# Two heads on halves of TensorE's array, one item for the compressed branch, and GpSimd on part of the probabilities

## The chip, the cores and the metric

The kernel runs on one core of one Trainium2 chip. Its time is the device time of one execution in microseconds. TensorE is called PE below, its weight loads PEld, VectorE DVE, ScalarE ACT, GpSimd POOL, and the queue that issues most DMAs SP. The profile is one execution recorded by the hardware profiler.

## The reference

The function is two blocks, one after the other, on x of 256 tokens by 1024. The first block has two layers of feed-forward networks and a mixer each (a gated recurrence in one, latent attention in the other); the change leaves it alone. The second block has two layers, each a modulated norm, a projection of 1024 to 3864 columns, the hybrid attention below, an output projection and a gated residual. With 256 tokens, 8 "moba" heads of width 64 see their own keys under a causal mask, and 8 "NSA" heads in two groups of four share keys and values per group, in three branches that are weighted by sigmoid gates and added:

```python
s_own = jnp.einsum('hqd,hkd->hqk', q, k_own).astype(jnp.float32)           # moba: causal, minus slope * distance
s_c = jnp.einsum('gjqd,gtd->gjqt', qg, kcb).astype(jnp.float32)            # compressed: T = 15 keys for each group
p_c = jax.nn.softmax(s_c, axis=-1) * ok_c
o_c = jnp.einsum('gjqt,gtd->gjqd', p_c.astype(vcb.dtype), vcb)
o_n = g[..., 0:1] * o_c + g[..., 1:2] * o_s + g[..., 2:3] * o_w            # o_s selected, o_w window
y = jnp.concatenate([o_m * jax.nn.silu(zm), o_n * jax.nn.silu(zn)], axis=-1)
return y @ w_out
```

At this length all 4 blocks of the selected branch are chosen and the window covers all keys, so both are plain causal attention with their own keys and values.

## The kernel before

Activations lie as features on 128 partitions by 256 tokens. Weights stream from memory in chunks of 128 x 2048; ACT rounds each half of a chunk (128 x 1024) to fp32r (`hi`, L688) and DVE forms the rest (`lo`, L1717), and a product of the large projections is three fp32r matmuls (L1049 to L1051). The order on each engine is written out by hand, and engines wait on counted steps of one another; nothing reorders it.

The change is in the second block, whose two layers run one after the other. After the projection each layer has an attention stage over a list `ITEMS`: 4 moba items, then for each of 4 pairs of NSA heads a window, a selected and a compressed item, 16 in all. An item is a pair of heads of width 64 that lie on partitions 0 to 63 and 64 to 127. Since the array is used whole, the keys of each head stand in a buffer that is zero in the other head's rows (`kmz`, `ksz`, `kwz`), and the values in one that is zero in the other head's columns (`vmz`, `vsz`, `vwz`). POOL writes these zeros at the layer's start (L643).

An item passes through these steps:

- PE, `scores_c`: for each of the two row tiles of 128 tokens, one fp32 matmul against both heads' keys (L1617: 256 columns for tile 0, 512 for tile 1) and one bf16 matmul that adds the bias (L1619). An fp32 matmul shows as two records, each with its own weight load.
- DVE, `maxima_c`: the negated row maxima, a reduction for each row tile (L2102).
- ACT, `exps`: four exponentials from PSUM, with sums (L928).
- DVE, `weigh_c`: reciprocal of the sums (L2111), for NSA times the gate (L2117), then four products in place (L2122).
- PE, `transposes_c`: six transposes (L1456). ACT copies the result to `ptC` (L935).
- PE, `values_c`: for each head 256 columns (L1650) and 128 columns (L1651), all fp32.
- After a pair's last item: DVE multiplies with z (L2293), ACT and DVE split the product (L1006, L2300).

A compressed item has 15 keys for each head: scores of 30 columns (L1607, L1609), four exponentials of 15 columns, four 16-row transposes (L1630) and products with 15 rows (L1645).

The loop on PE is, for item i: scores of i+2, values of i-1, transposes of i. On ACT: exps of i, in items 4 to 11 one half of the output weights, the two copies of i-1, the split of i-3. On DVE: weigh of i, the product of i-2, maxima of i+2, the split of i-3, in items 4 to 11 one half of the weights. In the last turns PE also takes the first parts of the output projection (`wout`), and the rest follows.

## Time and profile before

| what | value |
|---|---|
| median of 3 runs | 1602.69 us (1594.97 to 1605.1) |
| the profiled execution's own time | 1599.1 us |
| its span, first to last instruction | 1597.3 us |
| granted TensorE clock, mean | 0.983 |
| PE busy | 1519.2 us (95%), 12299 matmul records |
| DVE / ACT / POOL busy | 1105.5 / 779.5 / 202.8 us |
| attention stage, layer 0 | scores from 1301.90, last but one transposes end at 1360.32 us |
| attention stage, layer 1 | the same from 1499.07 to 1556.05 us |

The two stages make 115.4 us of the span. PE's busy time is not a measure of its work, since records overlap: the work of a group of matmuls is read from the start of one to the start of the next. A granted clock of 1.00 is the level of 2.4 GHz and 0.50 that of 1.2 GHz.

### The profile page before, as it was taken

The page shows a single profiled execution, that of the slowest core. Times are in us where ns is not written, and L with a number is a line of the kernel's source. Part 1 is how long each engine was busy: PE and PEld are TensorE (multiplying, and loading weights), DVE is VectorE, ACT ScalarE, POOL GpSimd, SP SyncE. Part 2 cuts the span into 40 slices and gives each one's busy share as a digit, 9 for nine tenths or more (in the row PEclk, how much of TensorE's full clock was granted, in tenths as well). Part 3 has the DMA queues.
Part 4 walks back from the last instruction along what each step waited for, and adds up shares of the span by engine and source line. Part 5 has one row for each costly group of instructions (what it writes and reads, how often), then busy time and mean ns, then how long its engine had stood idle before and what let it go on. Part 6 is the DMA issues. An engine that isn't in the chain of part 4 may idle for free.

```text
span 1597.3 us, 31108 instructions
## 1 busy us (share of the span) xinstructions
PE 1519.2 (95%) x12299; PEld 1460.1 (91%) x12299; DVE 1105.5 (69%) x1648; ACT 779.5 (49%) x1259; POOL 202.8 (13%) x239
## 2 busy tenths in 40 slices
PE   6999998989999989999999999999987998989998
PEld 6999998989999989999989799999977976889767
DVE  5886559966886586876677745976578448394583
ACT  5554375355544356544352634544364338254481
POOL 1111015601421010111010001101023000120000
PEclk9999999999999999999999999999998999999999
DMA  7787744325776645766645254876555503085010
GB/s 225 223 273 244 232 133 133 111 75 169 248 245 215 226 124 177 256 222 200 223 116 149 80 159 152 276 233 212 180 158 159 162 27 106 1 239 174 14 54 27
DMA packets 219309, 264.86 MB, mean 166 GB/s; under 512 B 22253, under 2 KB 197325, under 8 KB 219213
## 3 DMA queue, kind: packets, MB, share of 16 engines
q1 hardware_dynamic: 209136, 234.58, 47.0%
q0 software_dynamic: 8960, 27.37, 5.2%
q10 hardware_dynamic: 1117, 1.57, 0.3%
q8 instruction: 67, 1.10, 0.3%
q14 instruction: 29, 0.24, 0.0%
HBM read 262.44 MB, written 1.05 MB: 165 GB/s over the span
## 4 chain that ended last, share of the span: by engine, by line
PE 79%; DVE 11%; ACT 5%; DMA 2%; issue 1%; POOL 0%; SPq 0%; DVEq 0%; ACTq 0%
PE bank L1049 23%; PE bank L1051 23%; PE bank L1050 23%; DVE w_lo L1717 4%; PE bank L1617 2%; PE bank L1456 1%; PE bank L1650 1%; DVE rs L1729 1%; ACT w_hi L688 1%; DVE hg_s L1917 1%; PE bank L1470 1%; PE bank L1468 1%; PE bank L1063 1%; ACT sC L928 1%; DMA w_raw<-in_ffn_w_in 1%
## 5 line engine op out<-in xcount | busy, mean ns | idle before, releaser
L688 ACT ACTIVATE w_hi<-w_raw 128x1024 fp32r<-128x1024 f32 x452 | 454.3, 1039 | 466.0 <-PE bank L1051 312.4
L1049 PE MATMUL bank<-xh,w_lo 128*128 128x256 f32 x2312 | 652.5, 282 | 24.5 <-DVE xl L2176 14.2
L1717 DVE TENSOR_TENSOR w_lo<-w_raw,w_hi 128x1024 fp32r<-128x1024 f32 x452 | 549.4, 1251 | 148.5 <-ACT w_hi L688 147.4
L1050 PE MATMUL bank<-xl,w_hi 128*128 128x256 f32 x2312 | 647.8, 280 | 0.0
L1051 PE MATMUL bank<-xh,w_hi 128*128 128x256 f32 x2312 | 647.7, 280 | 0.0
L1049 PEld LDWEIGHTS bank<-xh,w_lo 128*128 128x128 f32 x2312 | 438.1, 189 | 28.9 <-DVE xl L2176 14.9
L1050 PEld LDWEIGHTS bank<-xl,w_hi 128*128 128x128 f32 x2312 | 437.4, 189 | 1.1 <-issue 0.7
L1051 PEld LDWEIGHTS bank<-xh,w_hi 128*128 128x128 f32 x2312 | 436.9, 189 | 0.3
L1049 PE MATMUL bank<-hh,w_lo 128*128 (+1 forms) x704 | 194.7, 277 | 0.0
L1050 PE MATMUL bank<-hl,w_hi 128*128 (+1 forms) x704 | 194.3, 276 | 0.0
L1051 PE MATMUL bank<-hh,w_hi 128*128 (+1 forms) x704 | 194.3, 276 | 0.0
L531 POOL DMA_DIRECT2D mod_raw<-in_w_ada x128 | 69.0, 543 | 529.6 <-DVE mod_acc L1749 401.8
L1050 PEld LDWEIGHTS bank<-hl,w_hi 128*128 128x128 f32 x704 | 132.1, 188 | 0.0
L1049 PEld LDWEIGHTS bank<-hh,w_lo 128*128 128x128 f32 x704 | 132.1, 188 | 0.0
L1051 PEld LDWEIGHTS bank<-hh,w_hi 128*128 128x128 f32 x704 | 132.1, 188 | 0.0
L1749 DVE SCALAR_TENSOR_TENSOR mod_acc<-mod_raw,csf,mod_acc 128x384 f32<-128x384 f32 x112 | 65.3, 619 | 38.0 <-DMA mod_raw<-in_w_ada 37.5
L610 POOL TENSOR_TENSOR sq<-sq 128x1024 f32<-128x1024 f32 x7 | 16.9, 2407 | 404.3 <-ACT sq L706 404.3
L699 ACT ACTIVATE xh<-X,col 128x256 fp32r<-128x256 f32 x72 | 30.4, 496 | 52.4 <-PE bank L1051 36.0
L928 ACT ACTIVATE sC<-bank,nmC 128x256 f32<-128x256 f32 (+2 forms) x128 | 48.0, 411 | 9.0 <-DVE nmC L2102 8.9
L653 POOL TENSOR_TENSOR y<-y,rs 128x512 f32<-128x512 f32 x4 | 6.9, 1738 | 355.6 <-DVE rs L1729 355.6
L1773 DVE TENSOR_TENSOR gate_t<-bank,rs 128x512 f32<-128x512 f32 x44 | 30.3, 689 | 27.7 <-PE bank L1051 27.6
L1781 DVE TENSOR_TENSOR up_t<-bank,rs 128x512 f32<-128x512 f32 x44 | 30.3, 688 | 24.7 <-PE bank L1051 24.7
(367 smaller groups left out, 2213.4 us busy)
## 6 DMA issues: line engine op xcount, KB each, us to landing
w_raw<-in_ffn_w_in SPq DMA_DIRECT2D x176, 512.0 KB, 4.7
w_raw<-in_ffn_w_out SPq DMA_DIRECT2D x88, 512.0 KB, 4.4
w_raw<-in_w_in SPq DMA_DIRECT2D x52, 512.0 KB, 4.5
mod_raw<-in_w_ada POOLq DMA_DIRECT2D x128, 192.0 KB, 4.4
w_raw<-in_a_w_in SPq DMA_DIRECT2D x32, 512.0 KB, 4.5
w_raw<-in_ple_w_gate SPq DMA_DIRECT2D x16, 512.0 KB, 4.5
w_raw<-in_b_w_out SPq DMA_DIRECT2D x16, 512.0 KB, 3.6
w_raw<-in_w_out SPq DMA_DIRECT2D x16, 512.0 KB, 3.5
```

The costliest lines, as they stand in the source:

```text
L531: pool.dma_start(mod_raw[:, n % 2, :], io["w_ada_2"][l][P * k:P * (k + 1), col:col + MOD_COLS]).then_inc(sem[f"mod_landed{n % 2}"], 16)
L688: A(w_hi[:, c % NSLOT, cols], w_raw[:, c % NRAW, cols], ACT.Copy).then_inc(*did(hi_ready))
L699: A(xh[:, k, :], X[:, k, :], ACT.Copy, scale=gain(k)).then_inc(*did(act_steps, ("xh", nu, k)))
L928: A(s[:, h, cols], src, ACT.Exp, bias=nm[:, 2 * t + h:2 * t + h + 1], accum_out=den[:, 2 * t + h:2 * t + h + 1]).then_inc(*did(act_steps, ...
L1049: mm(out, lhs[1], rhs[0], start=start, stop=False, skip_group_check=skip)
L1050: mm(out, lhs[0], rhs[1], start=False, stop=False, skip_group_check=skip)
L1051: return mm(out, lhs[0], rhs[0], start=False, stop=stop, skip_group_check=skip)
L1617: mm(bank[b][:, 0:2 * n], q[:, m, t * P:(t + 1) * P], kz[:, :, 0:n], start=True, stop=False)
L1717: V.tensor_tensor(w_lo[:, c % NSLOT, cols], w_raw[:, c % NRAW, cols], f32(w_hi[:, c % NSLOT, cols]), ALU.subtract).then_inc(*did(lo_ready))
L1749: V.scalar_tensor_tensor(acc, raw, cs, acc, ALU.mult, ALU.add).then_inc(sem["mod_steps"], 1)
L1773: V.tensor_tensor(gate_t[:, p % 2, :, :], two(bank[b][:, :]), rep(rs[:, :], 2), ALU.mult).then_inc(*did(gate_scaled))
L1781: V.tensor_tensor(up_t[:, p % 2, :, :], two(bank[b + 1][:, :]), rep(rs[:, :], 2), ALU.mult).then_inc(*did(up_scaled))
```

## The change

The keys and values no longer stand between zeros (`km`, `ksd`, `kwd`, `vmt`, `vst`, `vwt`). A score matmul has one head's 64 rows of queries and keys, and writes a PSUM bank of its own; a value matmul has one head's 64 output columns and writes 64 partitions. The shapes place them on row halves (64 x 128 at rows 0 or 64) and on column halves (128 x 64 at columns 0 or 64) of the array. The biases stay on the whole array, as four matmuls in place of two.

The compressed branch of all 8 heads and both row tiles is one item, the fifth of 13: one bias matmul, 8 score matmuls of 30 columns, one maximum, one subtraction, one exponential, one set of weights, two transposes, one copy. Its value product is a matmul with 32 rows inside each selected item (`vcz`, `ptK`); to this end the compressed values are computed for 4 copies of the 15 keys (`ghr`).

POOL multiplies the probabilities of row tile 1 of both heads (2 x 256 columns) by their weights, and DVE those of row tile 0 (2 x 128). The zeroing of the padded buffers is gone, and each of the copies into them is one instead of several.

```diff
 
-    ITEMS = [("moba", m, True, True) for m in range(4)]
+    ITEMS = [("moba", m, True, True) for m in range(4)] + [("cmp", 0, False, False)]
     for m in range(4):
-        ITEMS += [("win", m, True, False), ("slc", m, False, False), ("cmp", m, False, True)]
...
             pool.wait_ge(*when(("x", 9 + l, 3)))
-            for z in (kmz, vmz, ksz, kwz, vsz, vwz, kcz, vcz):
...
+
+            for i, (kind, _, _, _) in enumerate(ITEMS):
+                if kind != "cmp":
+                    item = ("c", l, i)
+                    pool.wait_ge(*when(("weight", item)))
+                    t1 = sC[:, i % 3, :, P:3 * P]
+                    G.tensor_tensor(t1, t1, rdC[:, i % 3, 2:4].unsqueeze(2).to_broadcast([P, 2, T]), ALU.mult).then_inc(*did(pool_steps, ("probs1", item)))
...
-                probs_t(("c", l, i), ptC[:, i % 2], 2 * P if kind == "cmp" else 3 * P)
+                item = ("c", l, i)
+                if ITEMS[i][0] != "cmp":
+                    return probs_t(item, ptC[:, i % 2], 3 * P)
+                act.wait_ge(*when(("pt", item)))
+                A(ptK[:, :], bank[4][:, 0:T], ACT.Copy).then_inc(*did(act_steps, ("ptcopy", item)))
...
-                exps(("c", l, i), 2 * (i % 2), sC[:, i % 3], nmC[:, i % 3], denC[:, i % 3], CMP_T if kind == "cmp" else None)
+                if kind == "cmp":
+                    act.wait_ge(*when(("max", ("c", l, i))))
+                    A(sC[:, i % 3, 0, 0:T], sC[:, i % 3, 0, 0:T], ACT.Exp).then_inc(*did(act_steps, ("exps", ("c", l, i))))
+                else:
+                    exps(("c", l, i), 2 * (i % 2), sC[:, i % 3], nmC[:, i % 3], denC[:, i % 3])
...
-            last.then_inc(*did(pe_groups, ("vcmp", l)))
+            pe.wait_ge(*when(("ghr", l)))
+            mm(bank[2][:, 0:DH], ghr[:, :], wc2[:, 2, :], start=True, stop=True).then_inc(*did(pe_groups, ("vcmp", l)))
...
                 if kind == "cmp":
                     take(b0)
+                    mm(bank[b0][:, 0:T], ident_bf[:, :], cbias[:, :, :, :].rearrange("p t h n -> p (t h n)"), start=True, stop=False, skip_group_check=True)
                     for t in range(TB):
-                        last = mm(bank[b0][:, t * 2 * CMP_T:(t + 1) * 2 * CMP_T], q[:, m, t * P:(t + 1) * P], kcz[:, g, :, 0:CMP_T], start=True, stop=False)
-
-                        last = mm(bank[b0][:, t * 2 * CMP_T:(t + 1) * 2 * CMP_T], ident_bf[:, :], cbias[:, 2 * m:2 * m + 2, t, :], start=False, stop=True)
+                        for mk in range(4):
+                            col = t * P + 32 * mk
+                            last = mm(bank[b0][:, col:col + 32].rearrange("p (h n) -> p h n", h=2)[:, :, 0:CMP_T], qs[:, mk, t * P:(t + 1) * P],
+                                      kcz[:, mk // 2, :, 0:CMP_T], start=False, stop=(t == 1 and mk == 3), skip_group_check=True)
                     last.then_inc(*did(pe_groups, ("s", ("c", l, i), 1)))
-                    release[b0] = ("exps", ("c", l, i))
+                    release[b0] = ("max", ("c", l, i))
...
-                kz = {"moba": kmz[:, m], "slc": ksz[:, g], "win": kwz[:, g]}[kind]
+                keys = {"moba": km[:, m], "slc": ksd[:, g], "win": kwd[:, g]}[kind]
+                for h in range(2):
+                    take(b0 + h)
+
                 for t in range(TB):
-                    b, n = b0 + t, (t + 1) * P
-                    take(b)
-                    mm(bank[b][:, 0:2 * n], q[:, m, t * P:(t + 1) * P], kz[:, :, 0:n], start=True, stop=False)
-
-                    mm(bank[b][:, 0:2 * n], ident_bf[:, :], bias[:, 2 * m:2 * m + 2, T - n:T], start=False, stop=True).then_inc(*did(pe_groups, ("s", ("c", l, i), t)))
-                    release[b] = ("exps", ("c", l, i))
+                    for h in range(2):
+                        rows_ = slice(h * DH, (h + 1) * DH)
+                        mm(bank[b0 + h][:, t * P:t * P + (t + 1) * P], q[rows_, m, t * P:(t + 1) * P], keys[rows_, 0:(t + 1) * P],
+                           start=(t == 0), stop=False, skip_group_check=True)
+                for t in range(TB):
+                    for h in range(2):
+                        last = mm(bank[b0 + h][:, t * P:t * P + (t + 1) * P], ident_bf[:, :], bias[:, 2 * m + h, T - (t + 1) * P:T],
+                                  start=False, stop=True, skip_group_check=True)
+                last.then_inc(*did(pe_groups, ("s", ("c", l, i), 1)))
+                for h in range(2):
+                    release[b0 + h] = ("exps", ("c", l, i))
...
             def transposes_c(i):
+                item = ("c", l, i)
                 if ITEMS[i][0] != "cmp":
-                    return transposes(("c", l, i), sC[:, i % 3])
...
+                    return transposes(item, sC[:, i % 3])
+                take(4)
+                pe.wait_ge(*when(("probs", item)))
+                for t in range(TB):
+                    last = nc.tensor.transpose(bank[4][:, t * P:(t + 1) * P], sC[:, i % 3, 0, t * P:(t + 1) * P], ident)
+                release[4] = ("ptcopy", item)
+                last.then_inc(*did(pe_groups, ("pt", item)))
...
                 kind, m, start, stop = ITEMS[i]
+                if kind == "cmp":
+                    return
...
-                o = bank[b][:, 0:T]
-                for h in range(2):
-                    if kind == "cmp":
-                        last = mm(o, vcz[0:CMP_T, g, h, :], ptC[0:CMP_T, i % 2, h, 0:T], start=False, stop=(h == 1), skip_group_check=True)
-                        continue
-                    v = {"moba": [vmz[:, t, 2 * m + h, :] for t in range(TB)],
-                         "slc": [vsz[:, t, g, h, :] for t in range(TB)], "win": [vwz[:, t, g, h, :] for t in range(TB)]}[kind]
-
-                    block0 = lambda: mm(o, v[0], ptC[:, i % 2, h, 0:T], start=(start and h == 0), stop=(stop and h == 1), skip_group_check=True)
-                    block1 = lambda: mm(o[:, P:T], v[1], ptC[:, i % 2, h, T:T + P], start=False, stop=False, skip_group_check=True)
-                    for product in ((block0, block1) if h == 0 else (block1, block0)):
-                        last = product()
+                for t in range(TB):
+                    for h in range(2):
+                        v = {"moba": vmt[:, t, 2 * m + h, :], "slc": vst[:, t, g, :], "win": vwt[:, t, g, :]}[kind]
+                        rows_, cols = slice(h * DH, (h + 1) * DH), slice(t * P, T)
+                        last = mm(bank[b][rows_, cols], v, ptC[:, i % 2, h, t * T:T + t * P], start=(start and t == 0), stop=(kind == "moba" and t == 1), skip_group_check=True)
+                if kind == "slc":
+                    rows_ = slice(32 * m, 32 * m + 32)
+                    last = mm(bank[b][:, 0:T], vcz[rows_, :, :].rearrange("p h d -> p (h d)"), ptK[rows_, :], start=False, stop=True, skip_group_check=True)
...
-            for which, kz in ((0, ksz), (1, kwz)):
+            for which, kd in ((0, ksd), (1, kwd)):
                 here, there = kA[:, 2 + which, :], bank[1][:, which * T:(which + 1) * T]
                 for g in range(GROUPS):
                     for h in range(2):
                         rows_ = slice(h * DH, (h + 1) * DH)
-                        V.tensor_copy(kz[rows_, g, h, :], (here if g == h else there)[rows_, :]).then_inc(*did(dve_steps, ("kB_used", l, 1)))
+                        V.tensor_copy(kd[rows_, g, :], (here if g == h else there)[rows_, :]).then_inc(*did(dve_steps, ("kB_used", l, 1)))
+            dve.wait_ge(*when(("gelu", l)))
+            for g in range(GROUPS):
+                V.tensor_copy(ghr[:, 64 * g:64 * g + 64].rearrange("p (a n) -> p a n", n=16)[:, :, 0:CMP_T],
+                              rep(gh[:, 30 + 15 * g:45 + 15 * g], 4)).then_inc(*did(dve_steps, ("ghr", l)))
             dve.wait_ge(*when(("kcmp", l)))
...
             for h in range(2):
-                V.tensor_copy(vcz[0:CMP_T, :, h, h * DH:(h + 1) * DH], bank[2][0:CMP_T, 0:P].rearrange("p (g d) -> p g d", g=GROUPS)).then_inc(*did(dve_steps, ("vcz", l)))
+                V.tensor_scalar(vcz[:, h, :], bank[2][:, 0:DH], const[:, C_HALF + h:C_HALF + h + 1], None, ALU.mult).then_inc(*did(dve_steps, ("vcz", l)))
...
                 dve.wait_ge(*when(("s", item, 1)))
-                for t in range(TB):
-                    V.tensor_reduce(nm[:, 2 * t:2 * t + 2], two(bank[b0][:, 30 * t:30 * t + 30]), AX.X, ALU.max, negate=True).then_inc(*did(dve_steps, ("max", item)))
+                if ITEMS[i][0] != "cmp":
+                    for t in range(TB):
+                        V.tensor_reduce(nm[:, 2 * t:2 * t + 2], twin[i % 2][:, :, t * P:t * P + (t + 1) * P], AX.X, ALU.max, negate=True).then_inc(*did(dve_steps, ("max", item)))
+                    return
+
+                rows16 = bank[2 * (i % 2)][:, 0:T].rearrange("p (a n) -> p a n", n=16)
+                nm16 = nmK[:, :, :].rearrange("p t h -> p (t h)")
+                V.tensor_reduce(nm16, rows16, AX.X, ALU.max, negate=True).then_inc(*did(dve_steps))
+                dve.wait_ge(*did.last)
+                dve.wait_ge(*when(("pt", ("c", l, i - 3))))
+                V.tensor_tensor(s_[:, 0, 0:T].rearrange("p (a n) -> p a n", n=16), rows16, nm16.unsqueeze(2).to_broadcast([P, 16, 16]), ALU.add).then_inc(*did(dve_steps, ("max", item)))
...
+                dve.wait_ge(*when(("exps", item)))
+                if kind == "cmp":
+                    s16 = s_[:, 0, 0:T].rearrange("p (a n) -> p a n", n=16)
+                    V.tensor_reduce(nmK[:, :, :].rearrange("p t h -> p (t h)"), s16, AX.X, ALU.add).then_inc(*did(dve_steps))
...
+                    dve.wait_ge(*did.last)
+                    V.tensor_tensor(s16, s16, rdK[:, :, :].rearrange("p t h -> p (t h)").unsqueeze(2).to_broadcast([P, 16, 16]), ALU.mult).then_inc(*did(dve_steps, ("probs", item)))
+                    return
+
+                V.reciprocal(rd[:, :], den[:, :]).then_inc(*did(dve_steps, ("weight", item)))
                 if kind != "moba":
-                    branch = {"cmp": 0, "slc": 1, "win": 2}[kind]
-                    gate = gates[:, :, :].rearrange("p t (h b) -> p t h b", b=3)[:, :, 2 * m:2 * m + 2, branch]
-                weigh(("c", l, i), sC[:, i % 3], denC[:, i % 3], rdC[:, i % 3], gate, kind == "cmp", CMP_T if kind == "cmp" else None)
+                    dve.wait_ge(*did.last)
+                    branch = {"slc": 1, "win": 2}[kind]
+                    V.tensor_tensor(two(rd[:, :]), two(rd[:, :]), gates4[:, :, 2 * m:2 * m + 2, branch], ALU.mult).then_inc(*did(dve_steps, ("weight", item)))
+                dve.wait_ge(*did.last)
+                for h in range(2):
+                    V.tensor_scalar(s_[:, h, 0:P], s_[:, h, 0:P], rd[:, h:h + 1], None, ALU.mult).then_inc(*did(dve_steps, ("probs", item)))
```

The order on PE before, one turn of the attention loop: scores of a selected item (`ksz`: its keys), value products of the selected item before (`ptC`, `vsz`: transposed probabilities and values), transposes of a compressed one.

```order
L1617 MATMUL bank<-ksz,qs 128x256
L1619 MATMUL bank<-bias,ident_bf 128x256
L1617 MATMUL bank<-ksz,qs 128x512
L1619 MATMUL bank<-bias,ident_bf 128x512
L1650 MATMUL bank<-ptC,vsz 128x256
L1651 MATMUL bank<-ptC,vsz 128x128 x2
L1650 MATMUL bank<-ptC,vsz 128x256
L1630 MATMUL bank<-const,sC 16x128 x4
```

The order on PE now, one turn in which the value products of a selected item come with the 32-row product of the compressed branch (L1682; `kwd`: keys of a window item, `vst`: values of the selected one):

```order
L1643 MATMUL twin<-kwd,qs 128x128 x2
L1643 MATMUL twin<-kwd,qs 128x256 x2
L1647 MATMUL twin<-bias,ident_bf 128x128 x2
L1647 MATMUL twin<-bias,ident_bf 128x256 x2
L1679 MATMUL twin<-ptC,vst 64x256 x2
L1679 MATMUL twin<-ptC,vst 64x128 x2
L1682 MATMUL twin<-ptK,vcz 128x256
L1478 MATMUL twin<-const,sC 128x128 x6
```

The order of the stages in a turn is the same; inside it the matmuls of the two heads alternate, and both row tiles' scores stand ahead of the biases.

The order on DVE before, the turn of the first selected item of a layer:

```order
L2111 RECIPROCAL rdC<-denC 128x4 [waits lo_ready,act_steps]
L2117 TENSOR_TENSOR rdC<-rdC,gates 128x4 [waits dve_steps]
L2122 TENSOR_SCALAR sC<-sC,rdC 128x128 [waits dve_steps]
L2122 TENSOR_SCALAR sC<-sC,rdC 128x256
L2122 TENSOR_SCALAR sC<-sC,rdC 128x128
L2122 TENSOR_SCALAR sC<-sC,rdC 128x256
L2293 TENSOR_TENSOR yC<-bank,zm 128x256 [waits dve_steps,pe_groups]
L2102 TENSOR_REDUCE nmC<-bank 128x2 [waits pe_groups] x2
L2300 TENSOR_TENSOR xl<-yC,xh 128x256 [waits act_steps]
L1717 TENSOR_TENSOR w_lo<-w_raw,w_hi 128x1024 [waits hi_ready]
```

And now, the turn of the first window item:

```order
L2315 RECIPROCAL rdC<-denC 128x4 [waits act_steps]
L2319 TENSOR_TENSOR rdC<-rdC,gates 128x4 [waits dve_steps]
L2322 TENSOR_SCALAR sC<-sC,rdC 128x128 [waits dve_steps]
L2322 TENSOR_SCALAR sC<-sC,rdC 128x128
L2332 TENSOR_TENSOR yC<-twin,zm 128x256 [waits dve_steps,pe_groups]
L2286 TENSOR_REDUCE nmC<-twin 128x2 [waits pe_groups]
L2286 TENSOR_REDUCE nmC<-twin 128x2
L2339 TENSOR_TENSOR xl<-yC,xh 128x256 [waits act_steps]
L1746 TENSOR_TENSOR w_lo<-w_raw,w_hi 128x1024 [waits hi_ready]
```

Two of the four products have left DVE for POOL, where in each layer, after its loads, stand twelve of them:

```order
L657 DMA wc_157<-in_w_cv_2 64x64
L664 TENSOR_TENSOR sC<-sC,rdC 128x2x256 [waits dve_steps] x12
L668 TENSOR_TENSOR y_168<-y_168,rs 128x512 [waits dve_steps]
```

Nothing but these twelve stands on POOL between the layer's loads and its end; the loads are ahead of them.

## Rows read from the trace of the kernel before

**Rows 1.** Busy us of PE, PEld, DVE, ACT, POOL by stretch; granted clock, DMA share, GB/s.

```profile
1301.90:1360.32 58.42, 53.01 (x282) 38.40 (x283) 46.82 (x153) 44.07 (x170) 0.00 (x0) 0.94 0.24 73
1360.32:1385.15 24.83, 24.83 (x210) 24.14 (x209) 2.65 (x7) 4.06 (x9) 0.00 (x0) 1.00 0.00 1
1499.07:1556.05 56.98, 53.16 (x282) 37.98 (x283) 46.97 (x153) 44.05 (x170) 0.00 (x0) 0.94 0.12 38
```

**Rows 2.** Instructions in order, PE, one turn of the loop: start us, us, what.

```profile
1327.20 0.82 PE L1456 MATMUL bank<-const,sC 128*128 128x128 f32 x6
1327.85 0.60 PE L1617 MATMUL bank<-ksz,qs 128*128 128x256 f32 x2
1328.29 0.27 PE L1619 MATMUL bank<-bias,ident_bf 128*128 128x256 bf16 x1
1328.39 1.02 PE L1617 MATMUL bank<-ksz,qs 128*128 128x512 f32 x2
1329.26 0.38 PE L1619 MATMUL bank<-bias,ident_bf 128*128 128x512 bf16 x1
1329.47 0.59 PE L1650 MATMUL bank<-ptC,vsz 128*128 128x256 f32 x2
...
1330.78 0.60 PE L1630 MATMUL bank<-const,sC 128*16 128x128 f32 x4
```

**Rows 3.** The chain that ended last, merged: the four exponentials of an item.

```profile
1329.23 1.61 ACT sC L928 x8
```

**Rows 4.** Instructions in order, ACT, two copies, one output copy, one weight half.

```profile
1328.05 0.87 ACT L935 ACTIVATE ptC<-bank 128x384 f32<-128x384 f32 x2
1328.81 0.42 ACT L1006 ACTIVATE xh<-yC 128x256 fp32r<-128x256 f32 x1
...
1330.70 1.08 ACT L688 ACTIVATE w_hi<-w_raw 128x1024 fp32r<-128x1024 f32 x1
```

**Rows 5.** Instructions in order, DVE, maxima to products of neighbouring items.

```profile
1329.77 1.02 DVE L2102 TENSOR_REDUCE nmC<-bank 128x2 f32<-128x256 f32 x2
1330.70 0.42 DVE L2300 TENSOR_TENSOR xl<-yC,xh 128x256 fp32r<-128x256 f32 x1
1331.03 1.22 DVE L1717 TENSOR_TENSOR w_lo<-w_raw,w_hi 128x1024 fp32r<-128x1024 f32 x1
1332.35 0.18 DVE L2111 RECIPROCAL rdC<-denC 128x4 f32<-128x4 f32 x1
...
1332.76 1.01 DVE L2122 TENSOR_SCALAR sC<-sC,rdC 128x128 f32<-128x128 f32 x4
```

**Rows 6.** Instructions in order, PE, a 15-row product between 128-row products.

```profile
1372.73 0.28 PE L1051 MATMUL bank<-xh,w_hi 128*128 128x256 f32 x1
1372.93 1.13 PE L1645 MATMUL bank<-ptC,vcz 15*128 15x256 f32 x4
1373.99 0.39 PE L1049 MATMUL bank<-xh,w_lo 128*128 128x256 f32 x1
1374.21 0.28 PE L1050 MATMUL bank<-xl,w_hi 128*128 128x256 f32 x1
```

**Rows 7.** Instructions in order, PE, from 128 output columns to 64.

```profile
1295.98 0.28 PE L1051 MATMUL bank<-xh,w_hi 128*128 128x256 f32 x1
1296.19 1.99 PE L1582 MATMUL bank<-win,wc 128*64 128x30 f32 x31
```

**Rows 8.** Instructions in order, DVE and POOL, products at the first layer's end.

```profile
1390.93 0.69 DVE L2327 TENSOR_TENSOR y<-y,rs 128x512 f32<-128x512 f32 x1
1390.99 3.44 POOL L653 TENSOR_TENSOR y<-y,rs 128x512 f32<-128x512 f32 x2 [177.52 <-DVE rs L1729]
...
1393.22 1.75 DVE L2327 TENSOR_TENSOR y<-y,rs 128x512 f32<-128x512 f32 x1
```

**Rows 9.** Busy time and granted clock in two single microseconds, columns as in Rows 1.

```profile
1301.00:1302.00 1.00, 0.29 (x5) 0.12 (x2) 0.77 (x5) 0.65 (x1) 0.00 (x0) 1.00 0.00 0
1302.00:1303.00 1.00, 1.00 (x4) 0.64 (x5) 0.00 (x0) 0.00 (x0) 0.00 (x0) 0.54 0.00 0
```

101 lines of the change are left out of this document (44 added, 57 removed).

## The prediction

> **What bounds the kernel now.** I read the windows by stage first. Each of the two attention stages runs from its first scores to the end of the last but one transposes: 58.42 us in layer 0 and 56.98 in layer 1 [rows 1]. In the first, PE is busy for 53.01 us, DVE for 46.82 and ACT for 44.07, so PE is ahead, and the two others are close behind: what PE gives up can be cashed only down to them. After the stage comes a stretch of 24.83 us with PE busy throughout [rows 1]; it is the output projection with the last value products in it, and has no stall to remove.
>
> Then the order of instructions, for PE's price of a turn. From start to start: six transposes 0.65 us, tile 0's scores 0.44 and bias 0.10, tile 1's scores 0.87 and bias 0.21, value products 1.31 [rows 2]. That is 3.58 us for an ordinary item. An fp32 record of 128 columns costs 0.11 us, one of 256 columns 0.215. A compressed item costs about 2.4: transposes 0.44, scores and biases about 0.7 (six records at the 0.11 that any record here costs at least), and value products 1.25, of which 0.39 is the price of 15-row matmuls between others that I read below [rows 6]. So PE has 12 x 3.58 + 4 x 2.4 = 52.6 us in a layer, of which some 49.7 lie before the stage's end; the other 7 to 9 us are stalls and low clock.
>
> ACT's price: four exponentials 1.61 us [rows 3], two copies 0.87, a half of the weights 1.08 (I take 1.0, since its end overlaps the next), an output copy 0.42 that costs 0.3 in a row with others [rows 4]. An ordinary item is 2.48, and 3.48 with a half.
>
> **The change on PE, ordinary items.** The score matmuls keep their columns, 768 in a pair of tiles, but two heads can now run on separate rows at a time. No row of this trace shows two matmuls on separate halves, so I bound it. Above: they go one after another, 0.44 + 0.87 = 1.31 as now. Below: they overlap. The records alternate as head 0, head 0, head 1, head 1, so a head's second record can go beside the other's first: 0.11 + 0.11 + 3 x 0.215 = 0.86; the eight weight loads at 0.11 give 0.9. I take 0.9, because a weight load and a matmul already overlap fully in the large stream, and nothing in the program orders one head behind the other. The same for the value products: 0.86 to 1.31, I take 0.9. Biases: four records of at most 0.10 for 0.31 before, 0.4. Transposes stay at 0.65.
>
> TensorE: Matmul & The Clock Gate in the Trainium skill (Part 3, Packing small matmuls) says that matmuls on different row groups start about 4 ns apart and measured 3.07 times the rate with four; by that both products would take 0.66 or little more. No run here shows it yet.
>
> **Price of the changes of shape.** From a 128-row matmul to four records with 15 rows and back, the starts are 1372.73 and 1374.21, 1.48 us apart. In between lie four records of 256 columns (0.86), one large-stream matmul before and one behind (0.115 each). 0.39 remains, 0.2 for each change of rows [rows 6]. From 128 output columns to 64 it is 0.21 between starts where 0.115 is usual, 0.1 [rows 7]. TensorEngine Tiling (Array Packing) in the Trainium skill (Tiling Modes, Key Properties) says that changing the mode drains the engine; it is the rule that speaks against this change, and the first of these rows agrees with it. Each turn of the loop now has two changes of rows and two of columns: 0.4 + about 0.1 = 0.5 us, between 0.4 and 0.8. An ordinary item is then 0.9 + 0.4 + 0.9 + 0.65 + 0.5 = 3.35 us, with ends at 2.8 and 4.2. The halves win little over 3.58 in ordinary items.
>
> **The compressed item.** One replaces four: a bias matmul 0.1, 16 score records at the 0.11 of a weight load 1.8, two transposes 0.22, and in the four selected items 0.43 + 0.2 each = 2.5. That is 4.6 in place of 9.6 us of PE, 5 us a layer. On ACT four times 1.0 + 0.6 or more of small exponentials and copies become one exponential and one copy of 256 columns, 0.7 (by the nearest copies [rows 4]); on DVE four short chains become one.
>
> **GpSimd and DVE.** The pool product has 512 columns a partition; the nearest row is 3.44 us for two such products, 1.72 each, between DVE's own [rows 8]. It starts when the weights are ready, 0.4 us after the exponentials, and PE's transposes wait for it. Behind them wait only ACT's copies. ACT does the next exponentials first, so the loop through POOL spans two items: weights 0.4, product 1.72, transposes 0.65, signals 0.2, copies 0.87 and the exponentials of the item after next 1.61 are 5.4 us, 2.7 for each item, below PE's 3.35. So this wait is hidden in the loop and costs once, at its end. But DVE pays: the same kind of product took it 0.69 alone and 1.75 beside POOL's [rows 8]. DVE's item was 0.41 + 1.01 + 0.93 + 0.33 for an output + 1.22 = 3.9 with a half [rows 5]; two of the four products, 0.5, go, and the two that stay may take 0.7 more, so 3.4 to 4.1. The end of the range is above ACT's 3.66.
>
> **The sum, for a layer.** The first item's exponentials end 5.9 us after the start (two microseconds of it at the low clock, which came after one in which PE was busy 0.29 [rows 9]); items 1 to 3 at 3.35, 10.0; the compressed item, where ACT has 2.5, 2.5; items 5 to 11 at 3.8, between ACT's 3.66 (3.48, and four output copies among seven) and DVE's upper end, 26.6; then weights 0.4, product 1.72, transposes 0.65 and signals, 2.9; and one more visit of the low clock, as each stage has now, 1.65. Sum 49.6 us. Against 58.42 and 56.98 that is 8.8 and 7.4. Behind the stage the value products save 0.4 twice but pay changes of shape and the 32-row product, +0.3 a layer. Ahead of it the two copies for `ghr` go beside PE's kcmp matmul; 0.1 a layer. The lighter projection copies, and the zeroing gone from POOL, are hidden: PE is full there, and ahead of it DVE's norm runs longer than POOL's zeros. Were that cover gone they could only help. Net 15.4 us, from the profiled execution's 1599.1 to 1583.7. The median of the runs is 3.6 us higher, 1602.7, and by it the sum is 1587.3. I forecast 1584.
>
> **Rivals.**
> - *The page's rule in full*: overlap at once and cheap changes, item 2.8. Then ACT sets items 5 to 11 at 3.66 and the loop through POOL items 1 to 3 at 2.7, -1.0 and -2.0; the first scores, with half the columns in time, start the exponentials 1.0 sooner, and PE's stage ends 0.8 sooner: 4.8 a layer, 1574. That it would run as separate heads 4 ns apart is the same page's statement as above. Against: the 0.39 of [rows 6].
> - *The halves do not overlap*: item 4.2 on PE, which binds throughout: 5.9 + 10 x 4.2 + 3.2 + 2.9 + 1.65 = 55.7; 2.7 and 1.3 us gained and about 1 lost behind: 1596. This is also the case that the change does not do what it says. For it: every fp32 matmul here is two dependent records.
> - *POOL and DVE hold each other up*: both stretch whenever they meet, DVE's item is 4.4 and POOL's product 2.5. Items 5 to 11 cost 4.2 more and the end 0.8: 10 in both layers, 1593. For it: 0.69 against 1.75 [rows 8]. Against: DVE's maxima read PSUM and fill much of that time.
> - *Slower: the clock.* PE is now less full and half its array idle. After a microsecond with PE at 0.29 the granted clock went to 0.54, near the lower level of 1.2 GHz [rows 9]. If that becomes usual in the stage an item costs about 1.8 times as much, 6.0 against 3.35. The gain of 8 us a layer is gone when 3 of 12 items are at the lower level, and the kernel is over 1% slower from 6 on; all of them: 5.9 + 10 x 6.0 + 3.5 + 3.5 = 72.9 in the stage, 15 over now, and 1 behind it, 1631. Against: with PE at some 90% of the time, idle stretches are short.
>
> **Chances.** Forecast 0.45, own range 1576 to 1591; the page's rule 0.22; no overlap 0.15; POOL and DVE 0.10; clock 0.08. A measurement of this kernel tells about 1% from no change, 16 us, so under 1586.7 counts as faster. Of the forecast 0.32 of its 0.45 lies there, with the page's rule 0.54; slower by over 1% is the clock and a bit of the two others, 0.09; within 1% 0.37. The range of 1569 to 1602 leaves out the clock, half of the lowest case and a little of the no-overlap case.
>
> **What the profile after would show.** The starts of one turn: head 1's first score record less than 0.1 us behind head 0's second (overlap) or 0.11 to 0.215 (none); a gap near 0.2 at each change of rows; an ordinary item's PE work at 3.35. Items 5 to 11 some 3.8 apart with ACT or DVE, not PE, at their head in the chain. POOL's products 1.2 to 1.8 us, DVE's `lo` at 1.22 or up to 2. The stretch behind the stage near 25. I am wrong if PE still leads the chain at over 4 us an item, or if the transposes' wait for POOL is long in ordinary turns.

## The result: 1626.5 us, slower by 1.5%, and the profile after

The changed kernel takes 1626.48 us (median of 4 runs, 1624.88 to 1627.71) against 1603.89 us for the kernel before (4 runs, 1594.97 to 1607.21): a ratio of 1.0149, 95% interval 1.0106 to 1.0192. The forecast was 1584, with a range from 1569 to 1602. Of the runs below, one of a_fix took 1888.68 us at a granted clock of 0.74; its median has that run in it, the ratios leave it out. The profiled execution took 1627.62 us, its span is 1625.8 us where it was 1597.3.

Where are the 28.5 us lost? The first scores of the first attention stage start at 1336.98 us in place of 1301.90: **35.1 us are gone before the attention that the change was meant to speed up begins**. From these scores to the end it is 288.8 us in place of 295.4, so behind them the change gains 6.6. Three stretches of the large matmul stream, all in the first block, which the change leaves alone, show where the 35 us go, with TensorE's rows alone (columns: stretch, its length, busy time with the number of records, granted clock, DMA share, GB/s). The kernel before:

```profile
30.00:130.00 100.00, 98.48 (x863) 1.00 0.77 248
400.00:480.00 80.00, 80.00 (x682) 1.00 0.78 248
520.00:570.00 50.00, 50.00 (x443) 1.00 0.55 181
```

The changed kernel:

```profile
30.00:130.00 100.00, 99.72 (x827) 1.00 0.76 242
400.00:480.00 80.00, 80.00 (x669) 1.00 0.77 246
520.00:570.00 50.00, 50.00 (x419) 1.00 0.65 207
```

PE is full in both, at a granted clock of 1.00, and yet it does 2 to 5% fewer records: in the third stretch one per 119.3 ns in place of 112.9. From the starts of successive 256-column records of the stream that read xh or xl, the mean spacing is 116.0 ns before and 119.9 after. Before, the trace has long stretches at 113.3 and others at 117.7; after, it is 120 nearly throughout. The page shows it too, in the mean of one matmul. Before, then after (columns: line, names, tile, shapes, count, busy us, mean ns, idle before):

```profile
L1050 PE MATMUL bank<-xl,w_hi 128*128 128x256 f32 x2312 | 647.8, 280 | 0.0
```

```profile
L1072 PE MATMUL twin<-xl,w_hi 128*128 128x256 f32 x2312 | 659.2, 285 | 0.0
```

3.9 ns on the 9528 records of three groups (three lines with 2312 + 704 + 160 each) are 37 us, of which most lie ahead of the first attention.

**In the attention** the stage now reads, from first scores to the start of the last group of six transposes, in both layers, against 58.08 and 56.71 us with 52.67 and 52.89 of PE before (beside [rows 1]; columns as there):

```profile
1336.98:1395.41 58.43, 49.64 (x377) 34.84 (x378) 46.67 (x96) 39.06 (x134) 12.46 (x12) 0.88 0.24 73
...
1531.48:1589.94 58.46, 49.64 (x376) 34.85 (x377) 46.66 (x96) 39.06 (x134) 12.46 (x12) 0.88 0.12 37
```

It seems to have gained nothing, but its end has moved: 48 records of the output projection now stand ahead of these transposes, where before none did. A fair stretch is from the first scores to the last matmul of the output projection: 82.97 and 81.54 us before, 77.30 and 77.33 after. One turn on PE, which answers to [rows 2]:

```profile
1372.85 0.84 PE L1478 MATMUL twin<-const,sC 128*128 128x128 f32 x6 [0.81 <-DVE sC L2322]
1373.62 0.93 PE L1643 MATMUL twin<-kwd,qs 64*128 64x128 f32 x8
1374.48 0.50 PE L1647 MATMUL twin<-bias,ident_bf 128*128 128x128 bf16 x4
1374.92 0.87 PE L1679 MATMUL twin<-ptC,vst 128*64 128x256 f32 x8
1375.72 0.69 PE L1682 MATMUL twin<-ptK,vcz 32*128 32x256 f32 x2
1377.12 0.84 PE L1478 MATMUL twin<-const,sC 128*128 128x128 f32 x6 [0.71 <-DVE sC L2322]
```

From start to start: transposes 0.77 with a change of shape, scores 0.86 with the next one, biases 0.44, values 0.80, that is 2.87 us. The 32-row product comes on top in selected items. The next transposes come 4.27 after the last, so PE stands idle. The score records of this turn alone, cut at their starts (PE busy with the records alive in it, then PEld):

```profile
1373.60:1373.64 0.04, 0.02 (x2) 0.02 (x2) 1.00 0.96 333
...
1373.82:1373.86 0.04, 0.04 (x4) 0.04 (x4) 1.00 0.76 256
...
1374.16:1374.19 0.03, 0.03 (x4) 0.00 (x0) 1.00 0.00 0
```

Two records begin within each of these windows of 30 to 40 ns (in the last two, the other records are the two that began before); in the trace the two heads start 6 to 7 ns apart. The next pair follows 0.10 us behind a pair of 128 columns and 0.21 behind one of 256, which is what a single record of that size costs in [rows 2]; only the first pair behind a change of shape takes 0.1 more. So the halves overlap in full.

The chain of waits, in an ordinary turn, is VectorE alone (start, us, what):

```profile
1366.13 1.14 DVE w_lo L1746
1367.27 0.10 DVE rdC L2315
1367.37 0.02 issue
1367.39 0.17 DVE rdC L2319
1367.57 0.03 issue
1367.59 1.36 DVE sC L2322 x2
1368.95 0.93 DVE nmC L2286 x2
```

Two products of 128 columns take 1.36 us; four, of 768 columns together, took 1.01 before [rows 5]. The timeline says why. The second row is GpSimd's product in the same turn, 128x512:

```profile
1371.34 1.17 DVE L2322 TENSOR_SCALAR sC<-sC,rdC 128x128 f32<-128x128 f32 x1
1371.38 1.04 POOL L664 TENSOR_TENSOR sC<-sC,rdC 128x512 f32<-128x512 f32 x1 [2.71 <-DVE rdC L2319]
```

DVE's product starts at 1371.34 and is over at 1372.51, 0.09 behind the end of POOL's. It is the same in all 24 meetings of the two layers: the first of DVE's two products begins 0.04 to 0.05 us ahead of POOL's, takes 1.16 to 1.17 and ends 0.08 behind it; the second takes 0.27 to 0.28.

### The profile page after: what moved, and what is told of

Its sections match the earlier page's. It is cut to its first block, busy times and chain, and to the rows that moved or that the text cites. A ratio compares the mean times of both kernels' runs of the same rounds, so it can differ in the third digit from the quotient of the medians.

```text
span 1625.8 us, 31086 instructions
## 1 busy us (share of the span) xinstructions
PE 1549.7 (95%) x12381; PEld 1491.1 (92%) x12381; DVE 1100.6 (68%) x1520; ACT 766.8 (47%) x1183; POOL 213.9 (13%) x251
## 4 chain that ended last, share of the span: by engine, by line
PE 81%; DVE 12%; ACT 3%; DMA 2%; issue 1%; POOL 0%; SPq 0%; DVEq 0%; ACTq 0%
PE twin L1071 24%; PE twin L1072 24%; PE twin L1073 24%; DVE w_lo L1746 3%; DVE sC L2322 1%; PE twin L1296 1%; DMA w_raw<-in_ffn_w_in 1%; DVE nmC L2286 1%; PE twin L1478 1%; DVE rs L1758 1%; PE twin L1492 1%; PE twin L1490 1%; PE twin L1085 1%; ACT xh L714 1%; PE twin L1679 0%
## 5 line engine op out<-in xcount | busy, mean ns | idle before, releaser
L1071 PE MATMUL twin<-xh,w_lo 128*128 128x256 f32 x2312 | 664.0, 287 | 20.4 <-DVE xl L2199 12.6
L1073 PE MATMUL twin<-xh,w_hi 128*128 128x256 f32 x2312 | 659.2, 285 | 0.0
L1072 PE MATMUL twin<-xl,w_hi 128*128 128x256 f32 x2312 | 659.2, 285 | 0.0
L1071 PEld LDWEIGHTS twin<-xh,w_lo 128*128 128x128 f32 x2312 | 448.0, 194 | 25.1 <-DVE xl L2199 13.6
L1072 PEld LDWEIGHTS twin<-xl,w_hi 128*128 128x128 f32 x2312 | 447.8, 194 | 1.0 <-issue 0.7
L1073 PEld LDWEIGHTS twin<-xh,w_hi 128*128 128x128 f32 x2312 | 447.5, 194 | 0.2
L1071 PE MATMUL twin<-hh,w_lo 128*128 (+1 forms) x704 | 199.6, 283 | 0.0
L1072 PE MATMUL twin<-hl,w_hi 128*128 (+1 forms) x704 | 199.2, 283 | 0.0
L1073 PE MATMUL twin<-hh,w_hi 128*128 (+1 forms) x704 | 199.2, 283 | 0.0
L1072 PEld LDWEIGHTS twin<-hl,w_hi 128*128 128x128 f32 x704 | 135.2, 192 | 0.0
```

The costliest lines, as they stand in the source:

```text
L1071: mm(out, lhs[1], rhs[0], start=start, stop=False, skip_group_check=skip)
L1072: mm(out, lhs[0], rhs[1], start=False, stop=False, skip_group_check=skip)
L1073: return mm(out, lhs[0], rhs[0], start=False, stop=stop, skip_group_check=skip)
```

## Experiments

Two questions: what slows the stream, and what each part gives in the attention. For the first there are three theories at the start: M, the place in memory of xh and of what lies behind it; S, PSUM in four tensors of two banks in place of eight of one; L, the length and place of the program's instructions. The table has for every kernel the distance of xh from the split weights, within 256 bytes of a partition (in the kernel before xh starts 106944 bytes behind w_hi, which is 192 more than a multiple of 256; xl and w_lo have the same remainders), the mean spacing of the stream's records on xh and xl, and two times of its profiled execution. Kernels b_ start from the kernel before, kernels a_ from the change.

| kernel | distance | spacing, ns | first scores at, us | from there to the end, us |
|---|---|---|---|---|
| before | 192 | 116.0 | 1301.9 | 295.4 |
| the change | 0 | 119.9 | 1337.0 | 288.8 |
| b_pad | 0 | 119.9 | 1333.4 | 303.2 |
| b_pad128 | 64 | 117.1 | 1316.3 | 298.6 |
| b_x64 | 0 (xh and xl alone) | 119.9 | 1319.5 | 303.2 |
| b_x32 | 160 | 118.2 | 1325.8 | 299.8 |
| b_x96 | 224 | 118.3 | 1323.2 | 301.2 |
| b_all64 | 192 | 115.7 | 1301.1 | 294.3 |
| b_twin | 192 | 115.2 | 1300.7 | 294.2 |
| a_align | 128 | 118.7 | 1325.7 | 288.4 |
| a_fix | 192 | 114.8 | 1299.6 | 283.2 |
| a_pad256 | 192 | 115.5 | 1304.8 | 283.2 |
| b_half | 192 | 116.0 | 1306.3 | 292.5 |
| a_nopool | 192 | 114.6 | 1293.3 | 276.8 |

### b_pad: the kernel before, with two unused columns

```
-C_N = C_LVL + P // 2 * len(LEVELS)
+C_N = C_LVL + P // 2 * len(LEVELS) + 2
```

> The kernel before, with two unused columns added to the constants' tile and nothing else. Theory M: starts in the large stream 120 ns apart everywhere, first attention at about 1337, time 1604 + 38 = about 1640. Theories S and L: as before, 1604, first attention at 1302.

Measured: 1639.13 us against 1598.76, ratio 1.0256 (1.0234 to 1.0278), first scores at 1333.4. The change's loss is there without the change, with every instruction as it was. Its tile of constants grew from 7168 to 7176 bytes, which the allocation rounds up to 7232, and every buffer behind it moved by 64 bytes. The rows of the same stretches are the change's rows:

```profile
30.00:130.00 100.00, 99.75 (x828) 1.00 0.76 243
400.00:480.00 80.00, 80.00 (x669) 1.00 0.77 246
520.00:570.00 50.00, 50.00 (x419) 1.00 0.62 203
```

### b_twin: PSUM in four tensors

```
-    bank = [nc.alloc_psum_tensor(f"bank{i}", [P, 512], F32) for i in range(8)]
+    twin = [nc.alloc_psum_tensor(f"twin{i}", [P, 2, 512], F32) for i in range(4)]
+    bank = [twin[i // 2][:, i % 2, :] for i in range(8)]
```

> The kernel before, with its PSUM as four tensors of two banks in place of eight of one; same addresses, same instructions. Theory S: starts 120 ns apart, first attention at about 1337, about 1640 us. Theories M and L: 113.3 and 117.7 ns, first attention at 1302, 1604.

Measured: 1596.65 us, one run, first scores at 1300.7. Theory S falls, and theory L fell with b_pad, where the instructions are those of the kernel before.

### a_fix: the change, with the old layout

```
-C_N = C_HALF + 2
+C_N = C_LVL + P // 2 * len(LEVELS)
...
+    half = place("half", [P, 2])
...
+            V.tensor_reduce(half[:, 0:1], const[:, C_LVL + P:C_LVL + P + P // 2:16], AX.X, ALU.add).then_inc(*did(dve_steps))
+            dve.wait_ge(*did.last)
+            V.tensor_scalar(half[:, 1:2], half[:, 0:1], -1.0, 1.0, ALU.mult, ALU.add).then_inc(*did(dve_steps))
```

> The change, except that the two half-mask columns are not part of the constants' tile: they are worked out by two small VectorE instructions a layer, into a tile behind all others, so that every buffer of the first block lies where it lay before. Theory M (memory place): the 35 us lost ahead of the first attention come from the 64 bytes by which the larger constants' tile shifts xh, xl and all behind it; the large stream's starts go back from 120 ns apart to 113.3 or 117.7, attention of layer 0 starts near 1302 instead of 1337, and the time is 1626.5 - 35 - 5 (the same cadence in the rest) = about 1587. Theory S (PSUM in four tensors of two banks): nothing returns, 1626. Theory L (length and place of the program's instructions): about 1626 too, or anything between, as the program's length is nearly that of the change.

Measured: 1588.95 us against 1598.76 (five of the six runs lie between 1585.09 and 1597.69), ratio 0.9939 (0.9907 to 0.9972); first scores at 1299.6. Theory M, and it lands on its number. The 35 us are back and what is left is what the change does in the attention. That this comes near the forecast of 1584 is partly luck, as the terms below show.

### b_pad128 and b_x64: how far, and which buffer

b_pad128 has `+ 32` in place of `+ 2`. b_x64 moves xh and xl alone:

```
+    base[0] += 64
     xh = fixed("xh", [P, KD, T], F32R)
     xl = fixed("xl", [P, KD, T], F32R)
+    base[0] += 448
```

> The kernel before, with 32 unused columns added to the constants' tile, so that all behind it shifts by 128 bytes. Theory M in the form in which the place within 128 bytes counts: as before, 1604. In the form in which the place within a larger piece counts, or the larger transfer itself: 120 ns, about 1640. Theories S and L: 1604.

Measured: 1616.66 us, one run, in between, which neither form of the expectation had: the cost isn't on or off, the size of the move counts.

> The kernel before, with xh and xl alone moved by 64 bytes (the place that gave 120 ns); everything behind them is moved by 512, which leaves its place within 512 bytes as it was. Theory X (the place of the moving operand counts): 120 ns between starts only where the stream reads xh and xl (from 21 to 260 us, and the input halves of the feed-forward, 360 to 504), and still 113.3 or 117.7 ns in the feed-forward's output at 504 to 574 us, which reads hh and hl, and where oh, cqh or hg_oh are read. Theory W (a buffer further ahead, such as constants, columns or ptok, counts, or the weights against the rest as a whole): nothing becomes 120 ns.

Measured: 1624.54 us, one run, against 1602.24. The records that read xh and xl are 119.9 ns apart, those on hh 115.6 and on oh 114.5. Theory X: what counts is the place of the operand that the stream reads at the time, and nothing further ahead. Its third stretch, the feed-forward's output, has 427 records where b_pad has 419; the two others are b_pad's:

```profile
30.00:130.00 100.00, 99.68 (x828) 1.00 0.75 242
400.00:480.00 80.00, 80.00 (x669) 1.00 0.75 240
520.00:570.00 50.00, 50.00 (x427) 1.00 0.65 206
```

### b_all64: own place, or distance to the weights

```
-    base = [(nc.sbuf_base + 63) // 64 * 64]
+    base = [(nc.sbuf_base + 63) // 64 * 64 + 64]
```

> The kernel before with every buffer moved by 64 bytes, the split weights w_hi and w_lo too. So far only what lies behind the weights was moved: by 0 the mean spacing in the stream was 116.0 ns, by 64 119.9, by 128 117.1, by 448 118.7. Theory A (the moving operand's own place counts; xh lies at 128 within 256 here, as in b_pad): 119.9 ns, about 1640. Theory R (its distance to the weights counts, 192 within 256 here as before): 116 ns, 1594 to 1607.

Measured: 1597.21 us, one run, beside 1595.82 for before. xh lies where it lies in b_pad, but the weights moved along, and nothing is lost: theory R. The first stretch has 867 records again:

```profile
30.00:130.00 100.00, 98.85 (x867) 1.00 0.78 251
```

SBUF — State Buffer in the Trainium skill (SBUF: two separate sides) says that within the engines' side only the port pair that VectorE and GpSimd share causes contention, and that PE never waits on anyone. These runs differ from that where both reads are PE's own: its weight loads and its moving operands. That no other reader or writer of memory is needed for the loss shows in the output projection of layer 0, where for 7.5 us no other engine works and no DMA moves data. The kernel before, then b_pad at the same place (columns: stretch, its length, PE, PEld, DVE, ACT, POOL, granted clock, DMA share, GB/s):

```profile
1375.50:1383.00 7.50, 7.50 (x69) 7.50 (x68) 0.00 (x0) 0.00 (x0) 0.00 (x0) 1.00 0.00 0
1407.90:1415.40 7.50, 7.50 (x65) 7.50 (x64) 0.00 (x0) 0.00 (x0) 0.00 (x0) 1.00 0.00 0
```

The starts in them are 113.3 and 120.0 ns apart. On the mean of the whole stream the distance costs up to 4 ns on each matmul, in this stretch 6.7. How the two reads meet no row shows.

### a_align, b_x96, b_x32: other places

a_align rounds the start of ptok, ahead of xh, up to 1024 bytes in a_fix; the two others put `base[0] += 32` and `base[0] += 480` there in the kernel before.

> The kernel a_fix with ptok, and so xh, xl and all behind them, moved by 448 bytes to a multiple of 1024. In the runs so far a place of 64 within 256 bytes gave stretches at 113.3 and at 117.7 ns, 128 gave 120.0 and 192 gave 117.7. Theory A1 (the best place is a multiple of 256 or more, as a 256-column fp32 row is 1024 bytes): 113.3 ns nearly everywhere; some 45% of 11,000 matmuls save 4.4 ns, 22 us, from 1588 to about 1567. Theory A2 (what counts is the distance to the weights' place, which is 128 within 256): it becomes 117.7 or more everywhere, 1600 to 1625. Theory A3 (the mix comes from the run and not from the place): as a_fix, 1588.

Measured: 1616.13 us against 1602.24, ratio 1.0084 (1.0057 to 1.0110). The round address is worse than the odd one (a_fix has 1588.95, in another comparison); with b_all64 theory A2 stands.

> The kernel before with ptok, xh, xl and all behind moved by 32 bytes, half of the step that cost 35 us. If the cost grows with the distance moved: about 118 ns, 1620. If pieces of 64 bytes count and 32 cuts them: 120 ns or more, 1640 or more. If it helps: 113.3 everywhere, 1580.

Measured: 1626.15 us, one run, against 1595.82.

> The kernel before with ptok, xh, xl and all behind moved by 480 bytes, so that xh lies at 32 within 512, 32 less than before. The same three cases as for 32 bytes more: between its neighbours at 0 (118.7 ns) and 64 (116.0), 117.4 ns and about 1615; cut pieces, 120 ns and 1640; or 113.3 ns and 1580.

Measured: 1627.36 us, one run, against 1595.82. Both spacings lie between those of their neighbours, but near the slower one: 118.3 ns between 116.0 at 192 and 119.9 at 0, and 118.2 between 118.7 at 128 and 116.0. So 32 bytes to either side of 192 cost some 30 us of the 40 that 64 bytes cost in b_pad. Of the six distances tried, 192 is the best, and none holds 113.3 ns throughout.

### a_pad256: the change with one number altered

```
-C_N = C_HALF + 2
+C_N = C_HALF + 64
```

> The change exactly, but for one number: the constants' tile has 64 columns more than before in place of 2, so that all behind it is moved by 256 bytes in place of 64. The distance of xh to the weights is 192 within 256 bytes, as before, and 448 within 512, where it was 192. Theory R256 (the distance within 256 counts): spacing 115 to 116 ns, first attention at about 1300, and 1588, as a_fix. Theory R512 (the distance within 512 counts): another spacing, 117 to 120 ns, 1610 to 1626. Theory N (the size of the constants' tile or its load costs): 1626.

Measured: 1593.63 us against 1599.62, ratio 0.9954 (0.9923 to 0.9985); from first scores to the end 283.2, as a_fix. The distance counts within 256 bytes, and 62 more unused columns are worth 33 us to the change (1626.5 to 1593.6, in different comparisons).

### b_half: the halves alone

```
-                    mm(bank[b][:, 0:2 * n], q[:, m, t * P:(t + 1) * P], kz[:, :, 0:n], start=True, stop=False)
+                    for h in range(2):
+                        rows_ = slice(h * DH, (h + 1) * DH)
+                        mm(bank[b0 + h][:, t * P:t * P + (t + 1) * P], q[rows_, m, t * P:(t + 1) * P], keys[rows_, 0:(t + 1) * P],
...
```

and the values and copies likewise, as in the change.

> The kernel before with one part of the change alone: keys and values not padded with zeros, the two heads' scores and values on halves of the array. The compressed branch stays four items of the whole array, and VectorE scales all the probabilities. Theory H (the halves bring most of what the change brings in the attention): TensorE's ordinary item falls from 3.58 to 2.8 us, 12 of them 9 us a layer, and the time from 1604 to about 1592. Theory D (VectorE and ScalarE are close behind, and the compressed items' merging brings most): VectorE's 46.8 us of the stage's 58.4 stay, so the stage ends 2 to 3 us earlier, and the time is 1598 to 1601.

Measured: 1600.94 us against 1602.24, ratio 0.9999 (0.9966 to 1.0032). Nearer to theory D, and its reason shows in the first two turns of layer 0 with a half of the weights (1322.83 to 1331.03 before, 1324.97 to 1333.16 here), both at a clock of 1.00: they last 8.20 us before and 8.19 here, though PE is busy 8.20 in the one and 7.10 in the other, for VectorE is busy 7.72 and 7.71 and ScalarE 8.15 and 8.19. The chain runs through VectorE alone in b_half's two. The clock adds something that neither theory had. The stages (PE busy, PEld, DVE, ACT, POOL, then the clock):

```profile
1306.33:1359.96 53.63, 46.58 (x351) 29.42 (x352) 45.80 (x148) 43.75 (x170) 0.00 (x0) 0.90 0.26 79
1499.44:1556.10 56.66, 50.50 (x351) 32.17 (x352) 46.90 (x153) 43.75 (x170) 0.00 (x0) 0.81 0.13 38
```

To the last matmul of the output projection the halves save 4.5 us in layer 0; in layer 1 they lose 1.0, and there the stage's mean granted clock is 0.81 where before it was 0.94. In 2-us pieces of that stage it reads 0.50 to 0.57, near the lower level of 1.2 GHz, in nine of 28. An idle stretch can go ahead of them (of 1526 to 1528, PE is busy 1.12, and the clock is at 0.55 in the next piece), but does not always lead to them (of 1516 to 1518 it is busy 0.97, and the clock stays at 1.00). That the clock is what ate the gain of layer 1 is likely and not shown by a run of its own.

### a_nopool: a_fix, with GpSimd's share given back

```
-                    G.tensor_tensor(t1, t1, rdC[:, i % 3, 2:4].unsqueeze(2).to_broadcast([P, 2, T]), ALU.mult)...
...
+                    for t in range(TB):
+                        cols = slice(t * P, P + t * 2 * P)
+                        V.tensor_scalar(s_[:, h, cols], s_[:, h, cols], rd[:, 2 * t + h:2 * t + h + 1], None, ALU.mult)...
```

> The kernel a_fix, with GpSimd's product of the second row tiles given back to VectorE as two products. In a_fix VectorE paces items 5 to 11 of the attention at 4.17 us: it does two products in 1.37, where four took 1.01 in the kernel before, and the transposes wait for GpSimd 8.6 us in the first stage. Theory P (the two engines slow each other, and the move costs more than it gives): VectorE's item falls to 1.01 + 0.93 + 1.13 + 0.42 + 0.3 = 3.8, eight items a layer save 0.4 and the chain to the transposes 0.5 once, so 1588 - 7 = about 1581. Theory G (the move relieves VectorE, as the prediction had it): items 0.25 longer, 1588 + 4 = 1592.

Measured: 1582.97 us against 1602.24, ratio 0.9885 (0.9837 to 0.9933), the lowest of all here (4 runs, 1571.91 to 1592.15). Its interval overlaps that of a_fix, 0.9907 to 0.9972; what sets the two apart is the traces. VectorE's four products take 1.01 us again, and a turn with them and one `xl` 3.73 (from one w_lo to the next, 1317.23 to 1320.96), where the same turn takes 4.08 in a_fix:

```profile
1317.23 1.13 DVE w_lo L1736
1318.37 0.10 DVE rdC L2308
...
1318.49 0.18 DVE rdC L2312
...
1318.69 1.01 DVE sC L2317 x4
1319.70 0.93 DVE nmC L2279 x2
1320.63 0.33 DVE xl L2334
```

```profile
1293.28:1346.38 53.10, 45.51 (x376) 31.39 (x377) 42.43 (x120) 38.99 (x134) 0.00 (x0) 0.97 0.27 81
```

From the first to the last of the stage's eight `w_lo` it is 25.79 us, where a_fix has 28.22. The granted clock is 0.97 (0.94 in layer 1), where it is 0.91 in a_fix. PE stands idle only a little less, 53.10 - 45.51 = 7.6 us where a_fix has 57.41 - 48.63 = 8.8, so why the clock is better is not shown. Theory P, whose 1581 it meets.

## Why the prediction was wrong

**Where the gain went.** From first scores to the last matmul of the output projection, for layers 0 and 1, the parts stack like this:

| step | layer 0, us | layer 1, us |
|---|---|---|
| before | 82.97 | 81.54 |
| + halves (b_half) | 78.43 | 82.52 |
| + one compressed item (a_nopool) | 71.07 | 72.54 |
| + products on GpSimd (a_fix) | 75.58 | 75.82 |
| + 64 bytes (the change) | 77.30 | 77.33 |

Each is one profiled execution. How far such times repeat is shown by kernels with the same attention: before, b_twin and b_all64 lie within 0.1 us in layer 0 and 0.9 in layer 1, a_fix and a_pad256 within 0.3 in both. So the compressed item brings 7.4 and 10.0, the halves 4.5 and -1.0, GpSimd's share costs 4.5 and 3.3, and the layout 1.7 and 1.5 here and 37 ahead.

- **The step that failed** is the one on what happens ahead of the attention: 0.1 us a layer for the two copies for `ghr`, the rest hidden. The sum has no term for the two mask columns (`C_HALF`) that the change adds to the constants, and so none for what they do to the addresses of everything that is placed after them; the large stream was taken to keep its pace. It went from 116.0 to 119.9 ns a matmul, and 35.1 us were lost ahead of the first scores. b_pad shows the columns alone: 31.5 us ahead of the first scores and 40 in all. None of the rivals had it; "slower: the clock" came to 1631, near the measured time, by a mechanism that did not cause it.
- **The sum in the attention was nearly right**: 58.42 + 24.83 = 83.25 before, and 49.6 + 25.1 = 74.7 forecast. a_fix has 75.6 where before has 83.0: 7.4 and 5.7 us gained, of 8.5 and 7.1. Its terms were off and cancelled in part: PE's item was priced 0.5 us too dear, which matters only where PE sets the pace, and the turns of items 5 to 11 were priced 0.4 too cheap.
- **PE's ordinary item**: 3.35 forecast, 2.87 measured. The starts of single records split it up: transposes 0.65, biases 0.34, scores and values 0.63 each, and 0.6 for the four changes of shape (0.1 between the last record of one shape and the first of the next, and up to 0.1 inside the first pair behind it). So the changes of shape were priced about right, at 0.5. The halves were not: I let the second head's records share only a part of their time and took 0.9 for each product. The rival "page's rule in full", with its 2.8, was right on PE. TensorE: Matmul & The Clock Gate in the Trainium skill (Part 3, Packing small matmuls) gives 4 ns between such starts; the trace has 6 to 7.
- **GpSimd and VectorE**: POOL's product was forecast at 1.72 us and took 1.04. I had added 0.7 to DVE's two products and taken an item between 3.4 and 4.1; I then took 3.8. The chain shows 3.75 without an output and 4.1 to 4.6 with one; the seven starts of transposes from 1360.4 to 1385.6 are 4.2 apart on average. I had also misread [rows 8]: the product of 0.69 us was not alone. POOL's first began 0.06 behind it and did not hold it, while the one of 1.75 met a POOL product under way. In the changed kernel DVE's first product is held in every meeting and lasts as long as POOL's: 1.17 beside 1.04. SBUF — State Buffer in the Trainium skill (Who interferes with whom) says that whichever of two such instructions issues first holds the shared port pair, and the other fully blocks; by that rule the product costs DVE what it costs POOL. The trace agrees on the cost; on the order it does not show it, since DVE's record starts 0.04 us ahead of POOL's each time and is still the one that is held, where the first of [rows 8], 0.06 ahead, was not. Why these differ stays open. The rival "POOL and DVE hold each other up", at 4.4 an item, was nearer than the forecast, though its 2.5 for POOL's product was not. Here the products are better left on DVE, as the turns of a_nopool show.
- **The clock**: the rival's mechanism is there at a far lower price than its 15 us a layer. The stage's mean went from 0.94 to 0.88; 0.06 of 58.43 us is 3.5 us of PE's work a layer at most, an estimate. And PE's weight loads wait 8.9 us for POOL's product in layer 0, in waits of up to 2.0:

```profile
PEld twin L1478 <- POOL sC L664: 8.9, 7, 2.0
```

- **The wait for POOL** was forecast as hidden in the loop. It is not: in the turns above PE stands idle ahead of each transposes. But DVE is the one that ends last: its second product is done 0.28 us behind POOL's. What PE's idle time costs by way of the clock was not measured apart.
- **What was right** is that PE does not set the pace of items 5 to 11: in the chain above VectorE does. Where an item comes with a half of the weights, the kernel before was near that already: the two turns that b_half leaves at 8.2 us show that taking work off PE alone bought nothing there.

## What to carry to other kernels

After a change, compare landmarks of the whole program and count records in stretches that it did not touch: a loss spread evenly over code that nobody edited points to layout. Put new constants and buffers behind those that a tuned stream reads, or pad so that they stay where they were, and time the padding alone. Before giving a second engine a share of a VectorE product, ask whether the two run at the same moment: if so the share may be paid twice, as here.

## What the runs showed of the hardware

- The distance between the moving operand and the weights in a partition, within 256 bytes, sets the pace of a full fp32r stream of 256-column matmuls: 119.9 ns at 0, 117.1 at 64, 118.7 at 128, 118.2 at 160, 114.6 to 116.0 at 192, 118.3 at 224. Up to 2.6% of this kernel's time hangs on it. The page shows only 5 ns more in the mean of one matmul (280 and 285): PE reads as full, at full clock, with either.
- At 192 the stream has two paces, 113.3 and 117.7 ns, and holds one for tens of microseconds: with the same layout, 400 to 480 us has 682 records in the kernel before and 702 in b_all64. This is likely why 16 runs of the kernel before on one chip reach from 1593.65 to 1610.32, and 4 of a_nopool, also at 192, from 1571.91 to 1592.15, while the 4 of the change and the 4 of b_pad, at distance 0, lie within 3 and 5 us. What sets the pace, and whether some layout holds 113.3 throughout, stays open.
- Two fp32 products of 64 rows on separate halves of the array start 6 to 7 ns apart and together take the time that one record of their size takes on the whole array, 0.10 to 0.11 us for 128 columns and 0.21 for 256; so do two of 64 output columns. Each change of shape adds 0.1 to 0.2.
- A DVE product of 128 x 128 that takes 0.27 us when POOL is idle takes 1.17 when it meets a POOL product of 128 x 512 that takes 1.04.
